# Gating bias written by ScalarE into reserved PSUM banks, a small gain table and unread products at the start, merge weights called three steps sooner, residual rows in another buffer

## The chip, the cores and the metric

One Trainium2 chip, 8 cores, one program on all of them. Each core takes one prompt sequence of 2048 positions and 16 sample sequences of 4 positions (64 rows); no core talks to another. The metric is the device time in microseconds of the slowest core. The kernel before took 1095.3 us (median of three runs).

## The reference, cut to what matters

```
xn = rmsnorm(h) * g_mix
proj = xn @ w_in                       # mixer A pair | u, v of mixer B | branch gates
glu = a_val * sigmoid(a_gate);  ca = causal depthwise conv (width 31) of glu
y_a = silu(layernorm(ca)) @ w_a_out
u, v = gelu(proj_u), gelu(proj_v)
v_n = layernorm(v) * ln_b_g + ln_b_b
s[t] = sum_s W_s[head][t, s] * v_n[s] + b_s[head][t]     # 128-position chunks, s <= t
y_b = (u * s) @ w_b_out
h = h + (sigmoid(g_a) * y_a + sigmoid(g_b) * y_b) @ w_out
h = h + ConvFFN(rmsnorm(h));  y = rmsnorm(h)
```

The outputs are y for prompt and sample rows, the carried convolution rows, and v_n of the sample rows (`o_vs`).

## The kernel before, in words

Everything on a core lives in one SBUF array (`arena`) with hand-set offsets; PSUM (`ps`) is eight banks, handed out in rotation by `rbank`. A small scheduler class writes one instruction list per engine, in program order, with semaphore waits where a buffer or bank is reused; so each engine is strictly first in, first out, and the order of the Python calls is the order on each queue. Weights (`w_all`, f32 in memory, bf16 in SBUF) come by DMAs that GpSimd issues; x, small tables and outputs by DMAs that SyncE issues. Every matmul is recorded under L303 (`mm`), every transpose under L313 (`tr`), ACTIVATE under L321, sum of squares under L318, two-tensor products under L324, tensor-scalar under L329 and L331, the three-input form under L334, DMAs under L180.

The stages in order of time:

- **Normalise and u.** 17 chunks of rows (16 of 128, the sample chunk of 64 is number 16). For each c: `sq` on ScalarE (needs x of c), `xscale` of c-1 on VectorE, `sq_rstd` of c (VectorE, then a power on GpSimd), transposes of c-1 on TensorE and `norm_evac` of c-1 on VectorE, which multiplies by the gain column 34 of the table `colA` (148 KB, loaded by SyncE after the second x). `PLAN[c]` says which u products (first column, width, column block j) run in step c; they need block j of the u weights and the normalised chunks.
- **v and the spatial mix.** Chunk 16 first, then 0 to 15. `v_mm` has 16 products of 512 columns and two Gelus into `vt` (f32); `v_stats` takes mean and 1/deviation; `v_center` is (v - mean) * gain on VectorE; `v_scale` on ScalarE multiplies by 1/deviation into `vn` (bf16). Two steps later `v_mix` puts the bias `Bm` into a bank by a product with the identity (512 columns, `start=True`), adds four products of 128 columns for four heads, twice per chunk, and VectorE multiplies u by the bank. `BmS` is the bias of the sample chunk, in one bank.
- **GLU** (32 steps of 16 products), with the sample rows' convolution on VectorE between.
- **Convolution.** For i = 0 to 15: for i below 8 a transposing step, then `conv(i)` (48 products of 128 columns, split over two banks) with coefficient matrices that `t_build` makes on GpSimd, ScalarE and VectorE three steps ahead; VectorE evacuates. `mload(4)` at i = 7 has GpSimd issue the loads of the first four merge blocks, gate and weight of mixer B for j = 0 and 1. They go to the last quarter of `Xc` (byte 25344 on), which conv(0) to conv(3) read. At i = 9, 11, 13 and 15 `run_fill(1)` runs one merge tile (`half_b`: 8 gate products, 8 weight products). From i = 8 on VectorE also takes LayerNorm statistics (`q_half`).
- **LayerNorm and transposes of mixer A** (`q_stats`, `q_z`, `q_tr`, with Silu on ScalarE), then the **merge** over j, then **w_out** (`wo_mm`): 17 chunks, each 16 products of 512, residual addition on VectorE with x rows in `xr` (three buffers at `OFF_C`, loaded by `xr_load`), sum of squares, scaling (`n2_scale`), and two steps later the transposes (`n2_tr`). The bytes of `xr` lie in `tbuf`, which the merge uses to its end. `u` (at `OFF_B`) is last read by `half_b` of j = 7.
- **ConvFFN** (22 blocks up, then down) and final norm, from 620 us to the end.

## Time and profile before

| what | value |
|---|---|
| median of the runs (lowest, highest) | 1095.3 us (1095.11, 1096.93) |
| the profiled execution's own time | 1095.86 us |
| its span, slowest core | 1094.2 us (cores: 1090.3 to 1094.2) |
| TensorE busy | 1064.1 us (97%) |
| VectorE, ScalarE, GpSimd busy | 630.7, 438.2, 181.4 us |
| mean granted TensorE clock, cores | 0.996 to 0.998 |

How to read it: all rows are of core 0, the slowest. PE is TensorE, PEld its weight loads, DVE VectorE, ACT ScalarE, POOL GpSimd, SPq the DMA issues of SyncE. In a timeline row the numbers are start and length in us, then engine, line, operation, output <- input, shape and count; the bracket says how long the engine had been idle before the first of them and what it waited for.

### The profile page before, as it was taken

To read this page: it belongs to the slowest core of one execution; us is meant where nothing else is said; L and a number is where in the kernel's file an instruction comes from. 1 tells how busy PE (TensorE), PEld (TensorE's weight loads), DVE (VectorE), ACT (ScalarE), POOL (GpSimd) and SP (SyncE) were. 2 spreads that over 40 slices of the span, in tenths; PEclk is the share of its full clock that TensorE was granted. 3 is DMA by queue.
4 is the path that set the end of the run, shared out by engine and by line. 5 is a ranking of instruction groups with operands and counts; after the bars stand their busy time and mean duration, and the time that the engine had idled before them with its cause. 6 is when DMAs were issued, how large, how long until landed. Compare 5 with 4: busy or idle time off the path is not lost.

```text
span 1094.2 us, 19114 instructions; the slowest of 8 cores (1090.3 to 1094.2 us)
## 1 busy us (share of the span) xinstructions
PE 1064.1 (97%) x6621; PEld 610.2 (56%) x6621; DVE 630.7 (58%) x1256; ACT 438.2 (40%) x800; POOL 181.4 (17%) x376
## 2 busy tenths in 40 slices
PE   5999999999899999999999999999999999999997
PEld 4764456666765555555545455555555555444444
DVE  4556987695988333333446666666666666333233
ACT  4644441123737411111155555555555555210111
POOL 3241113150631000100011111111111111000000
PEclk9999999999999999999999999999999999999999
DMA  9979014010240222142288623333223322543331
GB/s 211 268 102 166 1 26 87 2 30 1 35 78 2 40 39 37 28 73 39 49 248 273 175 40 58 59 58 50 50 50 56 59 49 40 138 145 116 116 109 65
DMA packets 36365, 89.40 MB, mean 82 GB/s; under 512 B 4080, under 2 KB 6256, under 8 KB 36272
## 3 DMA queue, kind: packets, MB, share of 16 engines
q0 software_dynamic: 21488, 38.74, 22.4%
q1 hardware_dynamic: 14784, 49.45, 14.0%
q8 instruction: 54, 0.88, 0.3%
q14 instruction: 39, 0.32, 0.1%
HBM read 108.57 MB, written 20.04 MB: 118 GB/s over the span
## 4 chain that ended last, share of the span: by engine, by line
PE 92%; DMA 2%; DVE 2%; ACT 1%; issue 1%; POOL 1%; SPq 0%; POOLq 0%; DVEq 0%; ACTq 0%
PE ps L303 90%; PE ps L313 2%; DMA arena<-x_p 2%; ACT arena L321 1%; DVE arena L334 1%; ACT arena L318 1%; DMA arena<-w_all 0%; POOL arena L331 0%; DVE arena L324 0%; DVE arena L604 0%; POOL arena L324 0%; SPq L180 0%; DVE arena L331 0%; DVEq L194 0%; POOLq L262 0%
## 5 line engine op out<-in xcount | busy, mean ns | idle before, releaser
L303 PE MATMUL ps<-arena 128*128 128x512 bf16 (+6 forms) x6077 | 1039.2, 334 | 9.6 <-DMA arena<-w_all 3.7
L303 PEld LDWEIGHTS ps<-arena 128*128 128x128 bf16 (+1 forms) x6077 | 577.6, 102 | 454.0 <-issue 20.5
L321 ACT ACTIVATE arena<-ps 128x512 f32<-128x512 f32 (+7 forms) x362 | 180.8, 513 | 295.0 <-PE ps L303 214.2
L334 DVE SCALAR_TENSOR_TENSOR arena<-arena 128x64 f32<-128x64 bf16 (+5 forms) x538 | 255.7, 511 | 34.6 <-POOL arena L324 14.5
L321 ACT ACTIVATE arena<-arena 128x512 f32<-128x512 f32 (+5 forms) x179 | 118.3, 673 | 195.5 <-DVE arena L334 171.9
L334 DVE SCALAR_TENSOR_TENSOR arena<-arena,ps 128x512 f32<-128x512 f32 (+4 forms) x120 | 69.9, 588 | 156.8 <-PE ps L303 147.8
L324 DVE TENSOR_TENSOR arena<-arena,ps 128x512 bf16<-128x512 f32 (+2 forms) x143 | 86.6, 615 | 83.9 <-ACT arena L321 83.5
L318 ACT ACTIVATE arena<-arena 128x1024 bf16<-128x1024 f32 (+3 forms) x53 | 54.2, 1022 | 152.4 <-DVE arena L324 132.9
L324 DVE TENSOR_TENSOR arena<-ps,arena 128x1024 bf16<-128x1024 bf16 (+4 forms) x71 | 64.0, 905 | 74.2 <-PE ps L303 66.5
L180 POOL DMA_DIRECT2D arena<-w_all x138 | 74.2, 549 | 192.1 <-PE ps L303 178.1
L321 ACT ACTIVATE arena<-ps,arena 128x512 f32<-128x512 f32 (+3 forms) x150 | 101.2, 705 | 4.4 <-PE ps L313 4.4
L324 POOL TENSOR_TENSOR arena<-arena 128x1 f32<-128x1 f32 (+2 forms) x73 | 42.1, 577 | 350.6 <-DVE arena L331 254.1
L331 DVE TENSOR_SCALAR arena<-arena 128x1 f32<-128x1 f32 (+4 forms) x81 | 25.4, 333 | 77.6 <-ACT arena L318 74.6
L331 POOL TENSOR_SCALAR arena<-arena 128x384 bf16<-128x384 bf16 x82 | 47.4, 596 | 96.1 <-PE ps L303 84.8
L341 POOL COPY arena<-arena 128x32 f32<-128x32 f32 (+1 forms) x66 | 13.9, 212 | 260.5 <-ACT arena L321 256.2
L313 PE MATMUL ps<-arena 128*128 128x128 bf16 (+2 forms) x544 | 40.9, 222 | 13.8 <-DVE arena L329 9.1
L313 PEld LDWEIGHTS ps<-arena 128*128 128x128 bf16 (+2 forms) x544 | 35.0, 100 | 23.0 <-issue 16.4
L334 DVE SCALAR_TENSOR_TENSOR arena<-ps,arena 128x512 f32<-128x512 f32 (+1 forms) x72 | 43.2, 642 | 5.1 <-DMA arena<-x_p 3.3
L324 DVE TENSOR_TENSOR arena<-arena 128x512 bf16<-128x512 f32 (+8 forms) x51 | 30.5, 597 | 8.4 <-ACT arena L321 2.2
L604 DVE BATCH_NORM_STATS2 arena<-arena 128x6 f32<-128x512 f32 (+1 forms) x34 | 23.5, 690 | 7.6 <-ACT arena L321 5.8
L329 DVE TENSOR_SCALAR arena<-arena 128x1024 bf16<-128x1024 f32 (+6 forms) x54 | 21.8, 413 | 4.6 <-POOL arena L324 2.3
L806 DVE BATCH_NORM_STATS2 arena<-arena 128x6 f32<-128x512 f32 (+1 forms) x34 | 21.4, 679 | 0.1
(17 smaller groups left out, 28.2 us busy)
## 6 DMA issues: line engine op xcount, KB each, us to landing
arena<-w_all POOLq DMA_DIRECT2D x138, 256.0 KB, 5.2
arena<-x_p SPq DMA_DIRECT2D x32, 512.0 KB, 7.4
h1s<-arena SPq DMA_DIRECT2D x16, 512.0 KB, 3.8
arena<-h1s SPq DMA_DIRECT2D x16, 512.0 KB, 4.2
o_yp<-arena SPq DMA_DIRECT2D x15, 512.0 KB, 2.9
o_ch<-st_a SPq DMA_DIRECT2D x1, 1664.0 KB, 18.7
arena<-dw_t POOLq DMA_DIRECT2D x4, 384.0 KB, 9.3
arena<-st_a POOLq DMA_DIRECT2D x1, 960.0 KB, 12.7
```

Source lines behind the costliest of these rows:

```text
L180: e.items.append(("op", lambda q, o=out, i=in_: q.dma_start(out=o, in_=i), stream, 16))
L303: S.op("pe", lambda q: q.matmul(out, lhsT=lhsT, rhs=rhs, start=start, stop=stop), [out], [lhsT, rhs], inc=stop)
L313: S.op("pe", lambda q: q.transpose(out=out, in_=in_, identity=ident), [out], [in_, ident], inc=inc)
L318: S.op("act", lambda q: q.activation(out=out, in_=in_, func=func, scale=scale, bias=bias, accum_out=accum), [out, accum], ins)
L321: S.op("act", lambda q: q.activation(out=out, in_=in_, func=func, scale=scale, bias=bias), [out], ins)
L324: S.op(en, lambda q: q.tensor_tensor(out=out, in0=in0, in1=in1, op=op), [out], [in0, in1])
L329: S.op(en, lambda q: q.tensor_scalar(out=out, in0=in0, scalar1=s1, scalar2=None, op0=op0), [out], ins)
L331: S.op(en, lambda q: q.tensor_scalar(out=out, in0=in0, scalar1=s1, scalar2=s2, op0=op0, op1=op1), [out], ins)
L334: S.op("dve", lambda q: q.scalar_tensor_tensor(out=out, in0=in0, scalar=scalar, in1=in1, op0=op0, op1=op1), [out], [in0, in1] + ([scalar] ...
L341: S.op(en, lambda q: q.tensor_copy(out=out, in_=in_), [out], [in_])
L604: S.op("dve", lambda q, i=i, a=a: q.bn_stats(out=s[:cs, 6 * i:6 * i + 6], in_=a), [s[:cs, 6 * i:6 * i + 6]], [a])
L806: S.op("dve", lambda e: e.bn_stats(out=s[:cs, 6 * hf:6 * hf + 6], in_=src[:cs]), [s[:cs, 6 * hf:6 * hf + 6]], [src[:cs]])
```

## The change

It does five things. The gain of the first norm comes from a table of its own, `colG` (4 KB), loaded second; `colA` follows the first eight x chunks. `warm(n)` puts n products of 128 columns of the identity into a bank that nobody reads, at five places of the first steps, and four u products of width 256 (block 2 to 5, columns 0 on) move one step later in `PLAN`. In the v stage `v_center` is gone: ScalarE does (v * rstd - mean * rstd) in place, GpSimd makes -mean * rstd and multiplies by the gain (`v_gain`), ScalarE writes the bias into a bank (`v_pre`; the first four by TensorE), banks 4 to 7 are kept for this and `rbank` turns over 0 to 3, the mix runs three steps behind instead of two, and the last three mixes stand among the first GLU steps. `vt` and `vn` turn by position in the order. The load of `b_dw` moves behind the last mix, so that of the carried rows `o_ch` no longer stands behind it. `mload(4)` is called at i = 4. `xr` moves from `OFF_C` to `OFF_B`.

```diff
...
     col_a = din("col_a", (128, 8, 37))
+    col_g = din("col_g", (128, 8, 1))
     col_f = din("col_f", (128, NFF, 4))
...
+        banks = [list(range(8))]
         def rbank():
-            b = bank_rr[0] % 8
+            b = banks[0][bank_rr[0] % len(banks[0])]
             bank_rr[0] += 1
...
-        def mm(out, lhsT, rhs, start, stop):
-            S.op("pe", lambda q: q.matmul(out, lhsT=lhsT, rhs=rhs, start=start, stop=stop), [out], [lhsT, rhs], inc=stop)
+        def mm(out, lhsT, rhs, start, stop, onto=False, inc=None):
+            S.op("pe", lambda q: q.matmul(out, lhsT=lhsT, rhs=rhs, start=start, stop=stop, skip_group_check=onto), [out], [lhsT, rhs],
+                 inc=stop if inc is None else inc)
...
         o += 384
+        colG = view(o, F32, (128, 8, 1))
+        o += 64
         M8 = view(o, F32, (128, 8))
...
         u_load()
-        xload(1)
+        S.dma("sp", colG, col_g)
+        for c in range(1, NXB):
+            xload(c)
         S.dma("sp", colA, col_a)
-        for c in range(2, NXB):
-            xload(c)
         mset(nh, -0.5)
...
-        def norm_evac(c, gcol):
+        def norm_evac(c, gcols):
             cs = rows(c)
             tt("dve", xnT[:, :, c * 128:c * 128 + cs], psb(nbank[c], BF16)[:, 0:8 * cs].rearrange("p (k t) -> p k t", k=8),
-               colA[:, :, gcol:gcol + 1].broadcast_to([128, 8, cs]), ALU.mult)
+               gcols.broadcast_to([128, 8, cs]), ALU.mult)
...
             xtr(c - 1)
-            norm_evac(c - 1, 34)
+            norm_evac(c - 1, colG)
...
             2: [(0, A1, (0, 1))],
-            3: [(128, A1, (0, 1)), (0, A2, (2,))],
-            4: [(0, A2, (3,)), (256, A1, (0, 1))],
-            5: [(384, A1, (0, 1)), (256, A2, (2,)), (0, A2, (4,))],
-            6: [(256, A2, (3, 4)), (0, A2, (5,))],
-            7: [(512, A2, (0, 1, 2))],
+            3: [(128, A1, (0, 1))],
+            4: [(256, A1, (0, 1)), (0, A2, (2,))],
+            5: [(384, A1, (0, 1)), (256, A2, (2,)), (0, A2, (3,))],
+            6: [(256, A2, (3,)), (0, A2, (4,)), (256, A2, (4,))],
+            7: [(512, A2, (0, 1, 2)), (0, A2, (5,))],
             8: [(0, A2, (6, 7)), (256, A2, (5, 6))],
...
         }
+        def warm(n):
+            b = rbank()
+            for i in range(n):
+                mm(psb(b)[:, 0:128], ident_b, ident_b, i == 0, i == n - 1)
         nstep(0)
...
         xscale(0)
+        warm(40)
         nstep_pe(1)
         sq_rstd(1)
+        warm(12)
         for c in range(2, 18):
...
                 u_mm(*p_)
+                if (c, n) == (2, 0):
+                    warm(18)
                 if n == 0:
                     nstep_pe(c)
+                if (c, n) in ((2, 1), (3, 1)):
+                    warm(12)
                 if c == 17:
...
         vstat = {}
+        vidx = {c: (c + 1) % 17 for c in CHUNKS}
...
                 for q in range(2):
-                    act(vt[c % 3][:64, q * 512:(q + 1) * 512], psb(b)[64 * q:64 * q + 64, :], AF.Gelu)
+                    act(vt[vidx[c] % 3][:64, q * 512:(q + 1) * 512], psb(b)[64 * q:64 * q + 64, :], AF.Gelu)
             for q in range(2) if c < 16 else ():
...
                     mm(psb(b)[:cs, :], xnT[:, k, c * 128:c * 128 + cs], vW[k][:, q * 512:(q + 1) * 512], k == 0, k == 7)
-                act(vt[c % 3][:cs, q * 512:(q + 1) * 512], psb(b)[:cs, :], AF.Gelu)
+                act(vt[vidx[c] % 3][:cs, q * 512:(q + 1) * 512], psb(b)[:cs, :], AF.Gelu)
...
             vstat[c] = s
-            t = vt[c % 3][:cs]
+            t = vt[vidx[c] % 3][:cs]
             layer_stats(s, [t[:, 0:512], t[:, 512:1024]], cs)
             layer_rstd(s, cs)
-        def v_center(c):
-            cs = rows(c)
-            s = vstat[c]
-            t = vt[c % 3][:cs]
-            stt(t, t, s[:cs, 12:13], lnbg[:cs], ALU.subtract, ALU.mult)
+            tsc("pool", s[:cs, 16:17], s[:cs, 12:13], s[:cs, 15:16], -1.0, ALU.mult, ALU.mult)
...
             cs = rows(c)
-            act(vn[c % 3][:cs], vt[c % 3][:cs], AF.Identity, scale=vstat[c][:cs, 15:16])
+            t = vt[vidx[c] % 3][:cs]
+            s = vstat[c]
+            act(t, t, AF.Identity, scale=s[:cs, 15:16], bias=s[:cs, 16:17])
+        def v_gain(c):
+            cs = rows(c)
+            t = vt[vidx[c] % 3][:cs]
+            tt("pool", vn[vidx[c] % 3][:cs], t, lnbg[:cs], ALU.mult)
             if c == 16:
-                stt(vso, vt[c % 3][:cs], vstat[c][:cs, 15:16], lnbb, ALU.mult, ALU.add)
+                tt("dve", vso, t, lnbg[:cs], ALU.mult)
+                tt("dve", vso, vso, lnbb, ALU.add)
                 S.dma("sp", o_vs, vso)
+        MB = [4, 5, 6, 7]
+        mbank = {}
+        mcount = [0]
+        def v_pre(c):
+            mbank[c] = []
+            for hf in range(2 if c < 16 else 1):
+                b = MB[mcount[0] % 4]
+                bias = Bm[:, 4 * hf:4 * hf + 4, :] if c < 16 else BmS
+                if mcount[0] < 4:
+                    mm(psb(b), ident_b, bias, True, True)
+                else:
+                    cp("act", psb(b).rearrange("p (a b) -> p a b", a=4 if c < 16 else 8), bias)
+                mcount[0] += 1
+                mbank[c].append(b)
         def v_mix(c):
-            cs = rows(c)
             if c < 16:
-                for hf in range(2):
-                    b = rbank()
-                    mm(psb(b), ident_b, Bm[:, 4 * hf:4 * hf + 4, :], True, False)
+                for hf, b in enumerate(mbank[c]):
                     for h4 in range(4):
...
                         o_ = psb(b)[:, h4 * 128:(h4 + 1) * 128]
-                        mm(o_, vn[c % 3][:, hd * 128:(hd + 1) * 128], WsT[:, hd, :], False, h4 == 3)
+                        mm(o_, vn[vidx[c] % 3][:, hd * 128:(hd + 1) * 128], WsT[:, hd, :], False, True, True, h4 == 3)
                     uu = u[:, 4 * hf:4 * hf + 4, c * 128:(c + 1) * 128]
...
             else:
-                b = rbank()
-                mm(psb(b), ident_b, BmS, True, False)
+                b = mbank[c][0]
                 for hd in range(8):
                     o_ = psb(b)[:, hd * 64:(hd + 1) * 64]
-                    mm(o_, vn[c % 3][:64, hd * 128:(hd + 1) * 128], WsTb[:, hd, :], False, hd == 7)
+                    mm(o_, vn[vidx[c] % 3][:64, hd * 128:(hd + 1) * 128], WsTb[:, hd, :], False, True, True, hd == 7)
                 uu = u[:, :, 2048:2112]
...
         order = [16] + list(range(16))
+        banks[0] = [0, 1, 2, 3]
         for i in range(len(order)):
...
             v_stats(order[i])
+            if i >= 1:
+                v_gain(order[i - 1])
+            if i >= 3:
+                v_mix(order[i - 3])
             if i >= 2:
-                v_mix(order[i - 2])
-            v_center(order[i])
+                v_pre(order[i - 2])
...
         gluS = view(OFF_D + 32768 + 8704, F32, (128, 8, 96))
-        S.dma("sp", bdw, b_dw.partition_broadcast(128))
         S.dma("sp", o_ch, st_a[:, :, 64:480])
...
+        glu(0)
+        v_pre(order[15])
+        v_scale(order[16])
+        v_gain(order[16])
+        v_mix(order[14])
         s_glu(1, (0,))
-        v_scale(order[16])
-        glu(0)
         v_mix(order[15])
+        v_pre(order[16])
         glu(1)
         v_mix(order[16])
+        bank_rr[0] %= 4
+        banks[0] = list(range(8))
+        S.dma("sp", bdw, b_dw.partition_broadcast(128))
         s_glu(1, (1,))
...
                 q_half(16, 1)
-            if i == 7:
+            if i == 4:
                 mload(4)
...
-        xr = [view(OFF_C + 4096 * i, F32, (128, D)) for i in range(3)]
+        xr = [view(OFF_B + 4096 * i, F32, (128, D)) for i in range(3)]
         h1 = [view(OFF_C + 12288 + 4096 * i, F32, (128, D)) for i in range(3)]
...
             trans8(xs2[i % 3], rows(c), nbank[c])
-            norm_evac(c, 35)
+            norm_evac(c, colA[:, :, 35:36])
...
         "col_a": np.ascontiguousarray(col.reshape(37, 8, 128).transpose(2, 1, 0)),
+        "col_g": np.ascontiguousarray(f(inp["g_mix"]).reshape(8, 128, 1).transpose(1, 0, 2)),
         "col_f": np.ascontiguousarray(colf.reshape(4, NFF, 128).transpose(2, 1, 0)),
```

## Rows read from the trace of the kernel before

**Rows 1.** The page, part 4: the chain that ended last, by engine.

```profile
PE 92%; DMA 2%; DVE 2%; ACT 1%; issue 1%; POOL 1%; SPq 0%; POOLq 0%; DVEq 0%; ACTq 0%
```

**Rows 2.** Waits of TensorE over the whole span: total us, times, longest us.

```profile
PE ps L313 <- ACT arena L321: 4.1, 3, 1.7
```

**Rows 3.** Timeline of the first 32 us, core 0.

```profile
7.73 1.06 ACT L318 ACTIVATE arena<-arena 128x1024 bf16<-128x1024 f32 x1 [1.39 <-DMA arena<-x_p]
...
10.54 1.23 DVE L324 TENSOR_TENSOR arena<-ps,arena 128x1024 bf16<-128x1024 bf16 x1 [2.22 <-DMA arena<-col_a]
...
13.86 1.06 ACT L318 ACTIVATE arena<-arena 128x1024 bf16<-128x1024 f32 x1 [4.98 <-DMA arena<-x_p]
...
17.36 1.06 ACT L318 ACTIVATE arena<-arena 128x1024 bf16<-128x1024 f32 x1 [1.60 <-DMA arena<-x_p]
...
18.25 3.38 PE L303 MATMUL ps<-arena 128*128 128x128 bf16 x24
...
30.59 1.03 PE L303 MATMUL ps<-arena 128*128 128x256 bf16 x8 [0.21 <-DVE arena L324]
```

**Rows 4.** Groups by shape, 110 to 140 us: busy us, mean ns, idle.

```profile
L303 PE MATMUL ps<-arena 128*128 128x512 bf16 x124 | 29.2, 379 | 0.0
...
L334 DVE SCALAR_TENSOR_TENSOR arena<-arena 128x1024 f32<-128x1024 f32 x7 | 8.9, 1278 | 0.0
...
L321 ACT ACTIVATE arena<-arena 128x1024 bf16<-128x1024 f32 x7 | 8.0, 1148 | 16.0 <-DVE arena L334 16.0
...
L321 ACT ACTIVATE arena<-ps 128x512 f32<-128x512 f32 x14 | 7.4, 582 | 0.0
```

**Rows 5.** Timeline of the v stage, ScalarE.

```profile
118.31 1.15 ACT L321 ACTIVATE arena<-arena 128x1024 bf16<-128x1024 f32 x1 [2.29 <-DVE arena L334]
...
122.71 1.15 ACT L321 ACTIVATE arena<-arena 128x1024 bf16<-128x1024 f32 x1 [2.29 <-DVE arena L334]
```

**Rows 6.** Groups of equal shape on GpSimd, whole span.

```profile
L331 POOL TENSOR_SCALAR arena<-arena 128x384 bf16<-128x384 bf16 x82 | 47.4, 596 | 96.1 <-PE ps L303 84.8 <-DMA arena<-dw_t 11.1
...
L324 POOL TENSOR_TENSOR arena<-arena 128x1 f32<-128x1 f32 x64 | 35.3, 551 | 304.0 <-DVE arena L331 241.5 <-DVE arena L329 62.5
```

**Rows 7.** Timeline of the convolution, 286 to 301 us.

```profile
286.19 0.58 POOL L180 DMA_DIRECT2D arena<-dw_t  x1 [0.60 <-ACT arena L321]
...
289.62 5.26 POOL L331 TENSOR_SCALAR arena<-arena 128x384 bf16<-128x384 bf16 x9 [2.86 <-PE ps L303]
...
294.83 2.17 POOL L180 DMA_DIRECT2D arena<-w_all  x4
...
300.29 5.89 PE L303 MATMUL ps<-arena 128*128 128x512 bf16 x27 [3.71 <-DMA arena<-w_all]
```

**Rows 8.** Window: busy (count) PE, PEld, DVE, ACT, POOL, clock, DMA, GB/s.

```profile
300.30:303.60 3.30, 3.30 (x8) 1.12 (x9) 1.99 (x4) 0.00 (x0) 0.09 (x1) 0.50 0.99 163
```

**Rows 9.** Timeline after the first merge tile, VectorE.

```profile
305.67 0.69 DVE L334 SCALAR_TENSOR_TENSOR arena<-arena,ps 128x512 f32<-128x512 f32 x1 [3.37 <-PE ps L303]
...
324.53 0.45 DVE L334 SCALAR_TENSOR_TENSOR arena<-arena,ps 128x288 f32<-128x288 f32 x1 [0.64 <-PE ps L303]
...
329.27 2.98 DVE L331 TENSOR_SCALAR arena<-arena 128x1024 bf16<-128x1024 f32 x4 [0.60 <-POOL arena L324]
```

**Rows 10.** Timeline of the w_out stage.

```profile
551.41 1.22 DVE L324 TENSOR_TENSOR arena<-arena 64x1024 f32<-64x1024 f32 x1 [2.17 <-ACT arena L321]
...
557.39 1.29 DVE L334 SCALAR_TENSOR_TENSOR arena<-ps,arena 128x512 f32<-128x512 f32 x2 [3.27 <-DMA arena<-x_p]
...
562.26 0.61 PE L313 MATMUL ps<-arena 128*128 128x128 bf16 x8 [1.45 <-ACT arena L321]
...
578.31 3.62 PE L303 MATMUL ps<-arena 128*128 128x512 bf16 x16
...
582.21 3.62 PE L303 MATMUL ps<-arena 128*128 128x512 bf16 x16
...
615.31 0.61 PE L313 MATMUL ps<-arena 128*128 128x128 bf16 x8 [1.74 <-ACT arena L321]
```

## The prediction

> **What bounds the kernel now.** First the page's chain that ended last [rows 1]: 92% of it is TensorE, so a change pays where it removes TensorE work or one of its few waits. Then the waits of TensorE and the timelines around them. There are four places. In the first 30 us x arrives late and the products run at half speed [rows 3]. In the v stage TensorE never waits [rows 4]; a chunk takes 122.71 - 118.31 = 4.40 us [rows 5], so only less TensorE work helps. In the convolution it stands still 3.71 us for the first merge block, and the next products run at half clock [rows 7, 8]. In the w_out stage it waits for ScalarE, 1.45 us at the start and 1.74 at the end [rows 10]; with one of 0.9 these make the 4.1 us of [rows 2]. A gain in one place can be eaten by the next engine in line; below I ask for it each time.
>
> **Front.** x of chunk 1 is there at 7.73, of chunk 2 at 13.86, of chunk 3 at 17.36 [rows 3]: an x takes 3.5 us, yet 6.13 lie between 1 and 2, so the table between them costs 2.6 us, and VectorE waited for it until 10.54. In these steps `norm_evac(c-1)` stands behind `sq_rstd(c)` on VectorE and so behind x of c. With `colA` last, x 2 to 7 come up to 2.6 us sooner. Against that, `colG` goes ahead of x 1: it costs between nothing and the same 2.6; it has as many rows of 32 bytes instead of 1184, and no weight load runs beside it yet, so I take 0.4. The product at 30.59, the first of step 7, waited for this chain and comes about 2.2 us sooner. But a product of width 256 and 8 blocks was moved into step 7. Eight products of 512 took 3.30 us at half clock [rows 8], 0.41 each, 0.21 at full clock, so the moved one is 8 x 0.1 = 0.9 us. Left: **1.3 us** (0 to 1.7). The loads of all eight x and `colA` are the same bytes, so x 8 comes no sooner, and the later steps are TensorE's own. On SyncE `colG` adds one issue before x 1.
> The 94 unread products cost 0.05 us each at full clock (a quarter of 0.21) and 0.10 at half, 5 to 10 us of TensorE, all in time in which it would wait for x: forty before the first transposes, the others in gaps of about a microsecond each. Their cover is the 3.5 us rhythm of x against some 1.4 us of work in steps 2 and 3. What they buy is speed: the 24 products from 18.25 are 4096 columns in 3.38 us, 1.2 columns per ns, the 1.2 GHz level. At 2.4 they take half, which matters only where TensorE and not x is late; so I count no gain for it, but without it the 2.2 us would shrink, since slow products would then be what x waits for.
>
> **v stage.** Removed: 33 bias products of 512 columns, four of which come back: 29. A chunk is 18 products of 512 and 8 of 128 in 4.40 us. A w_out chunk is 16 of 512 and 8 transposes of 128 in 582.21 - 578.31 = 3.90 [rows 10]. That is the new chunk, so a bias product is worth 0.25; by its columns alone 0.21. I take 0.235: 29 x 0.235 = **6.8 us** (6.1 to 7.3). Does another engine become the bound at 3.90?
> VectorE loses `v_center`, 1.28 per chunk [rows 4]: free.
> ScalarE has two Gelus of 0.58, `v_scale` 1.15 (same row, now into f32), and two bias writes of 512, nearest row the Gelu of 512, 0.58: 3.5 of 3.90. It holds until a bias write costs 0.8.
> GpSimd is the unknown. It has the power, 0.55 [rows 6], the new 128x1 product (at most the power's 0.55, I take 0.25), some 0.3 between instructions, and the gain product of 1024 f32 elements, of which no row exists. Below: 0.6 for 384 elements with one input [rows 6], in proportion 1.6 for 1024, or 1.3 if half of the 0.6 is fixed. Above: twice 1.6, for two inputs: 3.2. I take the middle, 2.2, so GpSimd is busy 3.3 of 3.90. The limit is 3.90 - 1.1 = 2.8.
> The Trainium skill, GPSIMD Engine Reference, § 3.1, gives a two-input f32 product 1.96 times VectorE's time; with VectorE's 1.22 for 1024 [rows 10] that would be 2.4, as an estimate, and the sum would not change.
> The added waits: the mix waits for GpSimd's product, which has the slack of the third step; the bias write waits for VectorE's multiply of the mix two chunks before, done a chunk earlier; behind it on ScalarE stands the next Gelu, with 0.4 us to spare. Four banks for `v_mm` are two chunks' worth. The tail (mixes among GLU steps) has one GLU step of cover for each. `o_ch` runs at the start of the stage instead of its end, beside GLU weights that are not needed before the stage is over: nothing. The second VectorE product for the sample rows (1.22) lies in VectorE's free time: nothing.
>
> **Merge blocks.** GpSimd idles 2.86 us until 289.62, after the coefficient load issued at 286.19 [rows 7]. conv(3) has by then been read, so the four issues, 2.17 us, go from 286.8 to 289.0: they fit, and no build is late. The load took 300.29 - 294.83 = 5.5 us to be usable; behind the coefficient load I allow 8 us: 295. The tile is due when conv(9) ends, 300.29 - 3.71 = 296.6. Gone then: 3.71 of wait, and the half clock: eight products in 3.30 where full clock needs 1.65 [rows 8]. Together 5.4. What is late next is VectorE: its evacuations run without pause up to the tile, and the first thing it could skip is its wait of 3.37 before 305.67 [rows 9], then small ones such as the 0.64 before 324.53. The LayerNorm products at 329.27 hang on that chain, and the transposes after them and Silu on ScalarE on these. So the gain is between 3.4 and 5.4; VectorE's rows give 3.4 + 0.6 + something: **4.3 us**. GpSimd's 2.17 us also leave the place between two builds.
>
> **Residual.** The first x rows were waited for 3.27 us by VectorE at 557.39 [rows 10]; their issue stood behind the last use of `tbuf`. `u` is free three columns of `half_a` sooner (j = 5, 6, 7), so all three loads land while the merge runs. The wait of 1.45 before 562.26 goes. The loop of evacuation, square, scale, transpose turned at TensorE's 3.90 with no slack, so the delay was carried to the end and came out as the 1.74 before 615.31: that goes too, but for about 0.2, since the last transpose follows scaling with only half a step between. **3.0 us** (1.5 to 3.2).
>
> **Sum.** 1.3 + 6.8 + 4.3 + 3.0 = 15.4. From the profiled execution's own 1095.86 (span 1094.2): 1080.5. The median of the runs is 0.6 lower, so **1080.0**.
>
> **Rivals.**
> *GpSimd bounds the v stage.* For: its product has no row, and it has only 0.6 us to spare. Against: 0.6 for 384 elements. At the upper bound of 3.2 a chunk takes 4.3, and 16 x 0.4 = 6.4 come back: 1086.4. Chance 0.10.
> *Slower than before: the same product, held up.* If it takes 4.6 us, a chunk takes 5.7 instead of 4.40, 16 x 1.3 = 21 us lost; with the 8.6 of the other parts, 1095 + 21 - 9 = 1107. It decides from a product of about 3.8 (chunk 4.9) on. The Trainium skill, SBUF — State Buffer, § Who interferes with whom, says that VectorE instructions with two SBUF inputs or in a two-port mode lock GpSimd out for their whole length. This is such a mechanism; here VectorE's mix reads one input from PSUM and its statistics have one input, so little would lock. The trace: nine GpSimd pieces beside VectorE's own pieces of the same builds took 5.26, 0.584 each, no more than the mean of 0.596 [rows 6, 7]. Chance 0.04.
> *VectorE eats the merge gain*, or the clock falls all the same: 2 instead of 4.3 us, 1082.3. Chance 0.09.
> *The early call does not load earlier* (the issues wait for something else, or land behind the coefficients after 300): 1084.3. Chance 0.04.
> *The front gives nothing or costs* (unread products in the way, u weights late): up to 2 us more than before, 1083.3. Chance 0.08.
> The forecast: 0.65.
>
> **Range and chances.** The low end has every upper bound: 1.7 + 7.3 + 5.4 + 3.2 = 17.6, and a little for what I left out, 1077.0. The high end takes in GpSimd as the bound: 1087.0. A measurement of this kernel tells about 0.2% (2 us) from no change. Faster 0.94, same 0.02 (the worst of the first rival's 0.10), slower 0.04 (the second rival).
>
> **What would show it.** v stage: chunk of 3.9 us, GpSimd product of 2 to 2.5, TensorE without a pause; wrong if TensorE waits for GpSimd or ScalarE. Convolution: no wait for `w_all`, clock 1.00 all through, GpSimd's four issues before the build of 289.62; wrong if a pause appears before conv(10) or the first `q_tr`. w_out: no VectorE wait for x, no TensorE wait of over 0.3. Front: x 2 at about 11.6, first product of step 7 near 28.4; wrong if TensorE waits for u weights there.

## The result, and the profile after

| | before | after |
|---|---|---|
| median of the runs | 1095.4 us | 1081.1 us |
| ratio, 95% interval | | 0.9865 [0.9847, 0.9882] |
| profiled execution, own time | 1095.86 us | 1081.38 us |
| spans of the cores | 1090.3 to 1094.2 us | 1078.6 to 1079.8 us |

The medians here and below are over all executions, slow ones in which the cores of one die ran at a lower granted clock included (one of after took 1111.6 us, the four others 1080.6 to 1081.4 with 1080.8 in the middle), while the ratios are of the undisturbed ones alone. The forecast was 1080.0 us, in a range of 1077 to 1087; by the median it was 1.1 us too low, by the 1080.8 it was 0.8. So 14.3 to 14.6 us were won where 15.4 were expected. The parts came out less evenly than their sum. Line numbers moved: `mm` is L306 now, `tr` L317, ACTIVATE L325, sum of squares L322, two-tensor products L328, tensor-scalar L333 and L335, the three-input form L338. In the kernels of the experiments they can be one to three lower.

The page of after (core 2, its slowest): the span, the busy times, and the chain that ended last.

```profile
span 1079.8 us, 19303 instructions; the slowest of 8 cores (1078.6 to 1079.8 us)
PE 1054.8 (98%) x6597; PEld 612.3 (57%) x6686; DVE 617.8 (57%) x1240; ACT 454.7 (42%) x829; POOL 227.3 (21%) x410
PE 93%; issue 2%; DVE 1%; DMA 1%; POOL 1%; ACT 1%; SPq 0%; POOLq 0%; DVEq 0%; ACTq 0%
```

TensorE still makes the chain [rows 1]. ScalarE is busy 16 us more and GpSimd 46 more, both beside it. The waits of TensorE on core 0, whole span (total us, times, longest us), against [rows 2]:

```profile
PE ps L306 <- DVE arena L345: 3.5, 1, 3.5
PE ps L317 <- ACT arena L325: 1.8, 2, 0.9
PE ps L306 <- DMA arena<-w_all: 0.5, 1, 0.5
```

The 3.5 is the very start, until the identity exists. The waits for ScalarE fell from 4.1 to 1.8, and the 3.71 for merge weights is gone (the 0.5 left is of u weights in the front).

**Where the time went.** Five marks cut an execution into stretches. In after, core 0, they are the first 64-row statistics, the first 24 products of the convolution, the table loads of Silu and of Gelu, and the issue for `st_f` at the end of w_out:

```profile
85.85 1.47 DVE L623 BATCH_NORM_STATS2 arena<-arena 64x6 f32<-64x512 f32 x2 [5.82 <-ACT arena L325]
319.81 1.28 ACT L325 ACT_TABLE_LOAD   x1 [2.94 <-PE ps L317]
534.64 1.28 ACT L325 ACT_TABLE_LOAD   x1
600.52 0.42 SPq L180 DMA_DIRECT2D arena<-st_f  x1
```

The mark between the first two is at 270.11 us. The same marks on all eight cores of each kernel give (means, lowest and highest core in brackets; the first column starts at 0, so it is the front):

| kernel | front | v and GLU | convolution to Silu | w_out | span, mean (highest) |
|---|---|---|---|---|---|
| before | 86.3 (85.7 to 86.9) | 191.57 | 53.85 (52.2 to 54.8) | 67.2 (66.7 to 68.4) | 1092.0 (1094.2) |
| after | 86.0 (85.9 to 86.2) | 184.35 (184.23 to 185.05) | 49.70 | 65.9 | 1078.9 (1079.8) |
| v stage alone | 86.4 (85.9 to 87.3) | 184.76 | 53.5 (51.5 to 55.1) | 68.2 (67.2 to 69.3) | 1086.4 (1089.5) |
| merge call alone | 86.9 (85.8 to 87.7) | 191.57 | 49.69 | 67.6 (66.9 to 68.8) | 1088.7 (1089.7) |
| residual rows alone | 86.6 (85.8 to 87.0) | 191.58 | 53.2 (51.9 to 55.2) | 65.5 | 1089.9 (1092.3) |
| front alone | 86.2 (85.7 to 86.7) | 191.63 | 53.7 (51.7 to 55.9) | 67.4 (65.7 to 69.0) | 1091.9 (1094.2) |
| all but the v stage | 86.9 (86.2 to 88.3) | 191.64 | 49.7 (49.7 to 50.0) | 65.55 | 1086.8 (1088.2) |
| before, gap filled | 86.8 (86.2 to 87.6) | 191.57 | 53.1 (52.6 to 53.9) | 67.2 (66.2 to 67.7) | 1091.6 (1093.4) |
| after, bias by TensorE | 86.7 (86.2 to 87.3) | 190.19 | 49.7 | 65.9 | 1085.4 (1086.1) |
| after, gain on VectorE | 86.8 (86.3 to 88.2) | 190.50 | 49.7 | 65.5 | 1085.5 (1086.8) |
| after, no unread products | 86.7 (86.3 to 87.1) | 184.23 | 49.7 | 65.9 | 1079.5 (1080.1) |
| after, plan of before | 86.9 (86.2 to 87.4) | 184.24 | 49.7 | 65.9 | 1079.6 (1080.1) |
| after, two-input product added | 86.8 (86.5 to 87.1) | 185.40 | 49.7 | 65.9 | 1080.7 (1081.0) |
| after, GpSimd's product twice | 86.7 (85.8 to 87.2) | 217.9 (217.3 to 218.9) | 49.7 | 65.9 | 1113.1 (1114.4) |

The merge, 214.8 us, and the rest after w_out, 478.1, are not in the table: they are the same in every kernel, but for the rest on three cores of "v stage alone", where it is 479.8.

Two things are to be seen. A stretch in which TensorE waits for no DMA has mostly one length on all eight cores, to some hundredths (v and GLU nearly everywhere; convolution and w_out wherever the edit is in). A stretch with such a wait differs by 2 to 4 us from core to core. And the metric is the slowest core, which in before was the one with the longest waits, core 0: on it the stretches give 0.70 + 7.31 + 5.05 + 2.47 = 15.5 us (forecast 15.4), on the mean of the cores 0.3 + 7.2 + 4.15 + 1.3 = 13.0. The slowest core of after is another one, core 2, so the result is 14.4 in spans.

Core 2 of after is an exception to the first: seven cores have 184.23 to 184.26 in v and GLU, and core 2 has 185.05. The view of its GLU steps shows what happened. VectorE's, GpSimd's and TensorE's timelines, core 2:

```profile
216.69 9.29 DVE L338 SCALAR_TENSOR_TENSOR arena<-arena 128x64 f32<-128x64 bf16 x1
```

```profile
216.87 9.03 POOL L335 TENSOR_SCALAR arena<-arena 128x384 bf16<-128x384 bf16 x16
```

```profile
227.70 5.37 PE L306 MATMUL ps<-arena 128*128 128x512 bf16 x23 [0.62 <-DVE arena L338]
```

One VectorE piece of 64 elements took 9.29 us and ended 0.08 after sixteen pieces of GpSimd that ran without a pause. The same pieces take some 0.6 us on core 0 beside the same row of GpSimd's. VectorE's evacuation came late, and TensorE waited 0.62 for it. On the 32 cores of before, after, "bias by TensorE" and "no unread products" this is the only piece of the GLU steps from 200 to 236 us that took over 2 us. What let it happen on one core wasn't tried.

### The profile page after: what moved, and what is told of

It reads as the page before. It is cut to its first block, busy times and chain, and to the rows that moved or that the text cites. A ratio compares the mean times of both kernels' runs of the same rounds, so it can differ in the third digit from the quotient of the medians.

```text
span 1079.8 us, 19303 instructions; the slowest of 8 cores (1078.6 to 1079.8 us)
## 1 busy us (share of the span) xinstructions
PE 1054.8 (98%) x6597; PEld 612.3 (57%) x6686; DVE 617.8 (57%) x1240; ACT 454.7 (42%) x829; POOL 227.3 (21%) x410
## 3 DMA queue, kind: packets, MB, share of 16 engines
q1 hardware_dynamic: 14928, 49.46, 14.6%
## 4 chain that ended last, share of the span: by engine, by line
PE 93%; issue 2%; DVE 1%; DMA 1%; POOL 1%; ACT 1%; SPq 0%; POOLq 0%; DVEq 0%; ACTq 0%
PE ps L306 90%; PE ps L317 3%; DMA arena<-x_p 1%; DVE arena L338 1%; ACT arena L325 1%; DVE arena L328 0%; POOL arena L335 0%; POOL arena L328 0%; ACT arena L322 0%; DVE arena L335 0%; SPq L180 0%; DVE arena L623 0%; POOLq L263 0%; DVEq L194 0%; DVE arena L345 0%
## 5 line engine op out<-in xcount | busy, mean ns | idle before, releaser
L306 PE MATMUL ps<-arena 128*128 128x512 bf16 (+6 forms) x6053 | 1029.8, 331 | 13.9 <-DVE arena L328 3.5
L306 PEld LDWEIGHTS ps<-arena 128*128 128x128 bf16 (+1 forms) x6142 | 580.7, 102 | 446.4 <-issue 12.8
L325 ACT ACTIVATE arena<-ps 128x512 f32<-128x512 f32 (+7 forms) x362 | 182.1, 514 | 301.7 <-PE ps L306 220.8
L338 DVE SCALAR_TENSOR_TENSOR arena<-arena 128x64 f32<-128x64 bf16 (+4 forms) x520 | 238.5, 494 | 32.9 <-POOL arena L328 13.0
L325 ACT ACTIVATE arena<-arena 128x512 f32<-128x512 f32 (+6 forms) x179 | 119.8, 681 | 158.1 <-DVE arena L338 133.5
L338 DVE SCALAR_TENSOR_TENSOR arena<-arena,ps 128x512 f32<-128x512 f32 (+4 forms) x120 | 69.7, 587 | 148.4 <-PE ps L306 140.9
L328 POOL TENSOR_TENSOR arena<-arena 128x1 f32<-128x1 f32 (+3 forms) x90 | 83.1, 925 | 296.5 <-DVE arena L335 251.5
L328 DVE TENSOR_TENSOR arena<-arena,ps 128x512 bf16<-128x512 f32 (+2 forms) x143 | 86.6, 615 | 83.9 <-ACT arena L325 83.9
L322 ACT ACTIVATE arena<-arena 128x1024 bf16<-128x1024 f32 (+3 forms) x53 | 54.2, 1022 | 151.8 <-DVE arena L328 132.9
L328 DVE TENSOR_TENSOR arena<-ps,arena 128x1024 bf16<-128x1024 bf16 (+4 forms) x71 | 64.0, 905 | 72.8 <-PE ps L306 65.8
L325 ACT ACTIVATE arena<-ps,arena 128x512 f32<-128x512 f32 (+3 forms) x150 | 101.2, 705 | 4.4 <-PE ps L317 4.4
L335 POOL TENSOR_SCALAR arena<-arena 128x384 bf16<-128x384 bf16 (+2 forms) x99 | 52.4, 545 | 96.9 <-PE ps L306 83.6
L335 DVE TENSOR_SCALAR arena<-arena 128x1 f32<-128x1 f32 (+4 forms) x81 | 25.8, 336 | 79.5 <-ACT arena L322 75.8
L317 PE MATMUL ps<-arena 128*128 128x128 bf16 (+2 forms) x544 | 40.1, 219 | 4.4 <-ACT arena L325 1.8
L338 DVE SCALAR_TENSOR_TENSOR arena<-ps,arena 128x512 f32<-128x512 f32 (+1 forms) x72 | 42.9, 640 | 1.8 <-PE ps L306 1.7
L317 PEld LDWEIGHTS ps<-arena 128*128 128x128 bf16 (+2 forms) x544 | 34.1, 98 | 14.1 <-issue 7.3
L328 DVE TENSOR_TENSOR arena<-arena 128x512 bf16<-128x512 f32 (+8 forms) x53 | 32.9, 621 | 8.7 <-ACT arena L325 2.2
L333 DVE TENSOR_SCALAR arena<-arena 128x1024 bf16<-128x1024 f32 (+6 forms) x54 | 21.8, 412 | 4.7 <-POOL arena L328 2.3
```

The lines of the kernel that those rows point to most:

```text
L306: S.op("pe", lambda q: q.matmul(out, lhsT=lhsT, rhs=rhs, start=start, stop=stop, skip_group_check=onto), [out], [lhsT, rhs], inc=stop if i ...
L317: S.op("pe", lambda q: q.transpose(out=out, in_=in_, identity=ident), [out], [in_, ident], inc=inc)
L322: S.op("act", lambda q: q.activation(out=out, in_=in_, func=func, scale=scale, bias=bias, accum_out=accum), [out, accum], ins)
L325: S.op("act", lambda q: q.activation(out=out, in_=in_, func=func, scale=scale, bias=bias), [out], ins)
L328: S.op(en, lambda q: q.tensor_tensor(out=out, in0=in0, in1=in1, op=op), [out], [in0, in1])
L333: S.op(en, lambda q: q.tensor_scalar(out=out, in0=in0, scalar1=s1, scalar2=None, op0=op0), [out], ins)
```

## The experiments

**One part at a time.** Four kernels from before, each with one part of the change as the diff ahead of the prediction shows it: the v stage, the call of `mload(4)`, the place of `xr`, and the front (`colG`, unread products, plan).

```diff
-            if i == 7:
+            if i == 4:
                 mload(4)
...
-        xr = [view(OFF_C + 4096 * i, F32, (128, D)) for i in range(3)]
+        xr = [view(OFF_B + 4096 * i, F32, (128, D)) for i in range(3)]
```

> The kernel before with the v stage alone changed (ScalarE bias writes, GpSimd gain product, kept banks, mixes three steps behind and spread, b_dw later). Main theory: each bias product taken from TensorE is worth 0.25 us, 29 of them 7.2 us, on every core alike, since no DMA is in it: about 1088.2, chunk of 3.9 us. Rival (the v stage's gain needs the earlier front, or part of it is given back in the GLU stage by VectorE): under 5 us, above 1090.5.

> The kernel before with the first merge loads called at i = 4 instead of 7. Theory A (the wait of 3.7 us and the half clock are the same on all cores): every core gains 5.0, 1090.4. Theory B (how long a load takes differs from core to core, so that the wait is a different one on each; in the kernel before the stretch from the first convolution to the Silu table took 52.2 to 54.8 us by core): the cores end up alike at 49.7 in that stretch, the mean gains 4.2, the slowest about 5; the time is between 1090.4 and 1091.5 and the spread of the cores' spans shrinks.

> The kernel before with the residual rows in the place of u. Theory A: both waits of ScalarE go on every core, 2.5 to 3 us: 1092.5. Theory B (only the cores whose x rows came latest had long waits; the stretch from the Gelu table to the load of the FFN history took 66.7 to 68.4 us by core): the stretch is 65.9 on all, the mean gains 1.3, core 0 gains 2.5; time 1093 to 1094.

> The kernel before with the front alone changed (small table, order of loads, unread products, four u products later). Main theory: x 2 comes 1 us sooner and the moved product takes 0.9 back: start of the v stage 0.3 us earlier in the mean of the cores, 0.7 on core 0; time 1095.0, no difference to be measured. Rival (the front is worth the 1.3 forecast): 1094.1.

Each set of experiments was run beside executions of before of its own (medians 1096.1 to 1097.0), so a time is to be read by its ratio.

| alone | median | ratio, 95% interval |
|---|---|---|
| v stage | 1091.6 us | 0.9956 [0.9938, 0.9974] |
| merge call | 1091.5 us | 0.9955 [0.9940, 0.9971] |
| residual rows | 1094.4 us | 0.9986 [0.9976, 0.9996] |
| front | 1096.0 us | 1.0001 [0.9991, 1.0011] |

The merge call and the residual rows do what their theories B said: their stretch gets one length on all cores (49.7, 65.5), and the mean gains less than core 0 does. The front alone moves nothing.

The v stage took its stretch from 191.57 to 184.76, 6.8 us on every core, near the 7.2 of its main theory, and yet only 0.44% off the time, 4.8 us, which is what the rival said. The other stretches tell why. On the mean of the cores w_out is 1.0 us longer than in before (68.2 for 67.2). TensorE's wait near its end is 2.1 us on seven of the cores, where before has 1.7 on all, and on three of these seven, cores 1, 2 and 3, the clock fell behind it. TensorE's timeline of the v stage alone, core 3, its slowest:

```profile
608.96 0.61 PE L316 MATMUL ps<-arena 128*128 128x128 bf16 x8 [2.08 <-ACT arena L324]
609.41 5.30 PE L305 MATMUL ps<-arena 128*128 128x512 bf16 x16
```

Sixteen products took 5.30 us where they take 3.62 [rows 10], and the granted clock of 610 to 613 us is 0.50. That is the 1.65 by which the rest after w_out is longer on these three cores. From core 0 of before to core 3 of this kernel the stretches give -6.8 in v and GLU, +0.7 in the front, +0.3 in the convolution, -0.6 in w_out and +1.6 behind it: -4.7, the 4.7 of the slowest spans (1094.2 to 1089.5). Why the wait near the end of w_out is longer with the v stage of after wasn't tried.

The single parts sum to 1.02% (11 us) where together they make 1.35%. With intervals of 0.1 to 0.2% on each the gap of 0.33% is itself only about as large as its uncertainty.

**All but the v stage.** Before, with the front, the merge call and the residual rows.

```diff
+        colG = view(o, F32, (128, 8, 1))
...
+            3: [(128, A1, (0, 1))],
...
-            if i == 7:
+            if i == 4:
                 mload(4)
...
-        xr = [view(OFF_C + 4096 * i, F32, (128, D)) for i in range(3)]
+        xr = [view(OFF_B + 4096 * i, F32, (128, D)) for i in range(3)]
```

> Before, with all parts of the change but that of the v stage: front, merge blocks, residual rows. It asks why the parts, each made alone, sum to 10.8 us where together they give 14.3. Theory A: the time is that of the slowest core, and each core waits for its DMAs by another amount; a part alone leaves the waits of the others, which pick another core as the slowest. With all three in, the cores end within about 1.5 us of each other, and the three are worth more than the 6.2 us of the single runs: 0.3 + 4.15 + 1.3 off the mean of the cores (1092.0) and the spread of 2.2 us above that mean gone to 0.9: 1087.1 span, 7.1 us, about 1088.3 us, ratio 0.9935, and 7.2 above after. Theory B: the v stage made alone meets something that it doesn't meet in after, and the others simply add: 6.2 us, ratio 0.9943, 1089.2.

1089.9 us, ratio 0.9937 [0.9924, 0.9951]. The interval holds both 0.9935 and 0.9943, so the time doesn't decide. The trace bears out a part of theory A: convolution and w_out have one length on the cores (49.7, one core 50.0, and 65.55), and the spread of the spans falls from 3.9 to 1.9 us. But the three single ratios sum to 0.58% and this kernel makes 0.63%, so these three simply add, as theory B says. What is worth more in company is the v stage: 0.44% alone, 0.72% as the difference between this kernel and after. In mean spans that is 5.6 us alone and 7.9 in company. In company its stretch gives 7.3, the front 0.9 (86.9 against 86.0, which no part of the v stage touches), and w_out takes 0.3 back. Alone, w_out and the fallen clock behind it took back 1.6. So theory B is right in this too: made alone, the v stage meets something that it doesn't meet in after, a wait of 2.1 near the end of w_out, which is 0.9 there.

**The bias by TensorE again.** After, one line changed.

```diff
-                if mcount[0] < 4:
+                if True:
                     mm(psb(b), ident_b, bias, True, True)
```

> After, with the bias of every chunk of the v stage written by the product with the identity again (29 more products of 512 columns); all else of the v stage (centring on ScalarE, gain on GpSimd, kept banks, the mix three steps behind, three mixes among the GLU steps) stays. Main theory: only the number of products sets the chunk, 29 x 0.235 to 0.25 = 6.8 to 7.3 us more, so 1088 us, ratio to before 0.993, the chunk 4.36 to 4.40 us, ScalarE with 1.2 us less per chunk. Rival: part of the 7.2 us that this stretch gained comes from the other edits (order, banks, the moved centring); then the time stays below 1086.

1087.8 us, ratio 0.9916 [0.9901, 0.9931]. That is 0.51% above after, 5.6 us; the stretch is 5.9 longer on seven cores and 5.1 on core 2, the one with the late piece in after. ScalarE's timeline in this kernel, core 0, gives the chunk:

```profile
115.44 1.23 ACT L325 ACTIVATE arena<-arena 128x1024 f32<-128x1024 f32 x1
119.77 1.23 ACT L325 ACTIVATE arena<-arena 128x1024 f32<-128x1024 f32 x1
```

4.33, and 4.33 to the next at 124.10. Against 3.90 in after that is 0.43 for two bias products, 0.22 each, close to the 0.21 by columns; 29 of them would be 6.3. Of the 0.4 missing from that, 0.13 is a pause between 150 and 155 us that after has and this kernel hasn't; the rest I didn't trace. So 5.9 of the 7.3 us of this stretch on core 0 are the products. The other 1.4 us, before's 191.57 against 190.19, come from the rest of the edit: before's chunk was 4.40 with the same count of products. TensorE's weight loads in before show a gap in each chunk:

```profile
118.01 1.18 PEld L303 LDWEIGHTS ps<-arena 128*128 128x128 bf16 x6
119.57 3.38 PEld L303 LDWEIGHTS ps<-arena 128*128 128x128 bf16 x23 [0.38 <-issue]
```

and this kernel has none there:

```profile
117.94 5.08 PEld L306 LDWEIGHTS ps<-arena 128*128 128x128 bf16 x30
```

16 x 0.07 us would be 1.1 of the 1.4. Which edit closes the gap (the kept banks, the mix three steps behind, the other order) wasn't tried alone. The time of 1088 is that of the main theory; the rival was right in that not all of the gain is the count of products, though not in its number, under 1086.

**The gain on VectorE.** After, with the product by the gain moved from GpSimd.

```diff
-            tt("pool", vn[vidx[c] % 3][:cs], t, lnbg[:cs], ALU.mult)
+            tt("dve", vn[vidx[c] % 3][:cs], t, lnbg[:cs], ALU.mult)
```

> The changed kernel with the gain product on VectorE instead of GpSimd. Main theory: VectorE then has 3.4 + 1.25 us per chunk, more than TensorE's 3.90, so a chunk takes 4.6 to 4.7 and the stage 16 x 0.75 = 12 us longer: 1093. Rival (the third step of slack hides it): 1081.

1088.4 us, ratio 0.9919 [0.9902, 0.9937]. The chunk is 4.35 (ScalarE's scaling at 112.59, 116.94 and 121.28), where the main theory had 4.6 to 4.7 and twice the loss: VectorE has 3.1 us of other work in a chunk, not 3.4. VectorE is the bound: its timeline over one chunk, core 0, is full,

```profile
114.35 0.21 DVE L626 BATCH_NORM_AGGREGATE arena<-arena 128x2 f32<-128x12 f32 x1
114.67 0.15 DVE L333 TENSOR_SCALAR arena<-arena 128x1 f32<-128x1 f32 x1
114.77 1.23 DVE L328 TENSOR_TENSOR arena<-arena 128x1024 bf16<-128x1024 f32 x1
115.92 1.28 DVE L328 TENSOR_TENSOR arena<-arena,ps 128x512 bf16<-128x512 bf16 x2
117.11 1.48 DVE L623 BATCH_NORM_STATS2 arena<-arena 128x6 f32<-128x512 f32 x2
```

0.21 + 0.15 + 1.23 + 1.28 + 1.48 = 4.35. And GpSimd's power, 0.55 in [rows 6], stands beside the product with both inputs in SBUF:

```profile
114.97 1.43 POOL L328 TENSOR_TENSOR arena<-arena 128x1 f32<-128x1 f32 x1 [2.48 <-DVE arena L333]
```

It began 0.2 us into that product and ended 0.4 after it. Giving GpSimd the product is what makes 3.90 possible; against VectorE it is worth 6.2 us of this stretch.

**GpSimd's product twice.** This goes at the rival that ended slower than before.

```diff
-            tt("pool", vn[vidx[c] % 3][:cs], t, lnbg[:cs], ALU.mult)
+            for _ in range(2):
+                tt("pool", vn[vidx[c] % 3][:cs], t, lnbg[:cs], ALU.mult)
```

> The changed kernel with the GpSimd gain product done twice. It measures from where on GpSimd bounds the stage, the second rival of the prediction. Main theory: GpSimd has 2 x 2.36 + 0.55 + 0.27 + 0.3 = 5.8 us per chunk, a chunk takes 5.8, the stage 16 x 1.9 = 30 us longer: 1111. Rival (other waits come on top, buffers of vt turning too slowly): over 1120.

1116.5 us, ratio 1.0181 [1.0159, 1.0203]. TensorE's timeline, core 0, then GpSimd's (two products and one power in a group of three):

```profile
122.23 4.06 PE L306 MATMUL ps<-arena 128*128 128x128 bf16 x23 [1.69 <-POOL arena L328]
```

```profile
117.13 5.35 POOL L328 TENSOR_TENSOR arena<-arena 128x1024 bf16<-128x1024 f32 x3
122.88 5.35 POOL L328 TENSOR_TENSOR arena<-arena 128x1024 bf16<-128x1024 f32 x3
```

A chunk takes 122.88 - 117.13 = 5.75, and TensorE stands still 1.7 in each. The mechanism of the rival is real: it had 5.7 for a product of 4.6 us, and with 4.7 us the kernel is slower than before by 20 us. Its turning point at 3.8 lies between the 2.36 and the 4.7 and wasn't measured. The time came between what the two theories say. On core 0 the stretch is 33.4 us longer than in after. TensorE's sixteen waits for GpSimd sum to 29.9 us. Each costs some 0.16 more than the wait itself (a chunk grows by 1.85, the wait is 1.7), together about 2.4. And behind the last and longest, 3.77, the granted clock is 0.68 from 185 to 190 us, which costs 1.6.

**A product with two SBUF inputs beside GpSimd's.** After, with an unread product on VectorE in each chunk.

```diff
             tt("pool", vn[vidx[c] % 3][:cs], t, lnbg[:cs], ALU.mult)
+            tt("dve", view(OFF_D + 65536, F32, (128, 256)), lnbg[:, 0:256], lnbg[:, 256:512], ALU.mult)
```

> After, with one unread product of 256 columns with both inputs in SBUF on VectorE for each chunk of the v stage (some 0.35 us, so VectorE has 3.5 of 3.9 busy). It asks whether GpSimd stands still beside such an instruction. If it does, GpSimd's product of 2.36 us, or the power of 0.55 if that is beside it, takes about 0.35 us longer, and both stay as they are if not. In either case TensorE has no wait and the time stays at 1081, since GpSimd then has 3.6 of 3.9 busy.

1082.6 us, one run; the chunk stays at 3.90. In the steady chunks the piece fell between GpSimd's instructions: the power took 0.59 to 0.60 instead of 0.55, the product 2.37. There the case tells nothing. At the start of the stage they met. GpSimd's timeline, core 0, and VectorE's:

```profile
93.34 2.35 POOL L328 TENSOR_TENSOR arena<-arena 64x1024 bf16<-64x1024 f32 x1
...
99.87 3.05 POOL L328 TENSOR_TENSOR arena<-arena 128x1024 bf16<-128x1024 f32 x2
```

```profile
93.41 3.35 DVE L328 TENSOR_TENSOR arena<-arena 64x1024 f32<-64x1024 f32 x1 [0.17 <-DVE arena L328]
...
100.95 1.55 DVE L328 TENSOR_TENSOR arena<-arena 128x256 f32<-128x256 f32 x1
...
120.39 0.41 DVE L328 TENSOR_TENSOR arena<-arena 128x256 f32<-128x256 f32 x1
```

The product of the sample rows takes 1.22 in after; begun 0.07 after GpSimd's, it took 3.35, 2.28 until GpSimd's end and nearly its own time after. The piece of 256 took 1.55 beside GpSimd's product and 0.41 alone. So here it isn't GpSimd that loses but whichever began second, and it loses the whole rest of the other's instruction. The delay went through: TensorE waited 1.32 us for GpSimd at 102.37, against 0.32 in after, 1.0 of the 1.14 us by which the stretch grew on core 0. The Trainium skill, SBUF — State Buffer, § Who interferes with whom, states this rule both ways (whoever issues first holds the shared pair for the whole instruction); this trace and the 1.43 above agree. I had expected GpSimd to lose here, and 0.35 us; wrong in direction and size.

**The gap filled.** Before, with 60 unread products of the identity ahead of the first merge tile, so that the wait stays and the clock doesn't fall. The 60 products add nothing to the output.

```diff
+            if i == 9:
+                unread(60)
             if i in (9, 11, 13, 15):
                 run_fill(1)
```

> The kernel before with 60 unread products of 128 columns (3.4 us) between conv(9) and the first merge tile, so that TensorE works while it waits for the blocks; the loads stay at i = 7. Theory A (the wait costs twice, 3.7 us of standing and 1.65 of half clock behind it): the eight products from about 300 run at clock 1.00, the Silu table comes about 1.6 us sooner (stretch from the first convolution 52.2 in the mean instead of 53.85), time 1094.3 to 1095. Theory B (VectorE is late anyway, so the clock costs nothing): the clock is full and the stretch is unchanged.

1095.5 us, ratio 0.9991 [0.9981, 1.0000]. The windows of this kernel, core 0 (engine busy times; then PEclk, DMA share, GB/s):

```profile
300.00:304.00 4.00, 3.95 (x29) 2.11 (x28) 2.80 (x6) 0.60 (x1) 0.55 (x1) 1.00 1.00 121
```

The clock is 1.00 where [rows 8] has 0.50, and the tile is evacuated at 303.65 instead of 305.67 [rows 9]. Yet the time falls by about 1 us, at most 2, and the stretch, 53.1 on the mean of the cores, is between the 52.2 of theory A and the 53.85 of theory B. All cores of the five kernels with the late call tell why. Core 6 of before waited for the same load; its timeline and its window:

```profile
300.43 3.78 PE L303 MATMUL ps<-arena 128*128 128x512 bf16 x19 [3.49 <-DMA arena<-w_all]
```

```profile
300.40:303.70 3.30, 3.27 (x16) 1.53 (x17) 2.25 (x5) 0.60 (x1) 0.34 (x1) 1.00 1.09 140
```

Almost the same pause as on core 0 (3.49 for 3.71), the same 3.30 us, but 16 products at the 2.4 GHz level where core 0 has eight at 1.2. Its convolution stretch is 3.17 us longer than the 49.70 of after, core 0's is 5.05. In before and the three single-part kernels with the late call, 32 cores in all:

| clock in the 3.3 us after the pause | cores | pause | stretch over 49.70, less the waits for `w_all`: median (lowest, highest) |
|---|---|---|---|
| 0.50 to 0.69 | 19 | 2.3 to 4.2 us | +1.35 (+1.1 to +2.5) |
| 1.00 | 13 | 2.2 to 3.5 us | -0.34 (-0.6 to +0.7) |

On six of the cores with the full clock a second, short wait of 0.2 to 0.7 us for the next block follows; it is taken off too. So a pause that leaves the clock alone costs 0.34 less than its length, and a fall of the clock costs 1.7 on top, the 1.65 that [rows 8] holds. VectorE swallows nothing beyond that 0.34. How long the pause was doesn't by itself say which happens, since the two kinds overlap from 2.3 to 3.5 us. The 60 products take 3.2 us themselves: in this kernel four cores stand at 2.86 over after without any wait, the others at 3.4 to 4.2 with one of 0.4 to 1.0. They help the cores whose clock would have fallen and cost the others something, and the slowest core gains little.

**No unread products.** After, `warm` doing nothing.

```diff
             b = rbank()
-            for i in range(n):
+            for i in range(0):
```

> The changed kernel without any unread product. Theory A (they give the first 20 us the full clock, and it matters): the first transposes take 1.0 us instead of 0.6, products fall behind x, the v stage starts 1 us or more later: 1082 to 1083. Theory B (x is the bound and the half-clock products fit between its arrivals): v stage starts within 0.3 us of 86.0: 1081.1.

1081.8 us, ratio 0.9865 [0.9849, 0.9880], the ratio of after itself. Timeline of TensorE, core 0, of this kernel, then of after:

```profile
8.47 1.01 PE L317 MATMUL ps<-arena 128*128 128x128 bf16 x8 [8.47 <-DVE arena L333]
...
16.59 1.06 PE L317 MATMUL ps<-arena 128*128 128x128 bf16 x8
...
29.82 1.03 PE L306 MATMUL ps<-arena 128*128 128x256 bf16 x8 [0.96 <-DVE arena L328]
```

```profile
8.47 0.61 PE L317 MATMUL ps<-arena 128*128 128x128 bf16 x8 [0.58 <-DVE arena L333]
...
16.05 0.61 PE L317 MATMUL ps<-arena 128*128 128x128 bf16 x8
...
29.02 1.03 PE L306 MATMUL ps<-arena 128*128 128x256 bf16 x8 [0.18 <-DVE arena L328]
```

The unread products do what they are for: the first three transposing steps take 0.4 us less each, 0.61 for 1.01. The prediction took products at half rate for the 1.2 GHz level by the 1.2 columns per ns; the granted clock of the profile reads 1.00 here in before, in this kernel and in after, so it does not bear that out, and what halves the rate stays open. But the v stage starts at 86.7 here and, in the seven kernels with after's whole front (the doubled product too), at 86.0, 86.2, 86.7, 86.7, 86.8, 86.8 and 86.9: no difference that this measurement can tell.

**The plan of before.** After, with `PLAN[3]` to `PLAN[7]` of before.

```diff
-            3: [(128, A1, (0, 1))],
-            4: [(256, A1, (0, 1)), (0, A2, (2,))],
+            3: [(128, A1, (0, 1)), (0, A2, (2,))],
+            4: [(0, A2, (3,)), (256, A1, (0, 1))],
...
-            7: [(512, A2, (0, 1, 2)), (0, A2, (5,))],
+            7: [(512, A2, (0, 1, 2))],
```

> After, with the plan of the u products of before (four groups of eight products of width 256 one step earlier, so one group less in step 7). Main theory (the 0.9 us that the prediction charges for the moved group): TensorE waits for x in steps 2 to 6 of after by 0.4 to 1.0 us in each, the group of width 256 fits there, and the products from step 7 on, which run without a pause, are eight fewer: the v stage starts 0.8 to 0.9 us sooner on every core, 1080.2 us. Rival: the weights of block 2 and the following ones are not there yet one step sooner, TensorE waits for them with the transposes behind it, and the start of the v stage stays or comes up to 2 us later, 1081 to 1083.

1081.7 us, ratio 0.9859 [0.9840, 0.9879]. The rival was right. TensorE's timeline, core 0:

```profile
17.12 2.15 PE L306 MATMUL ps<-arena 128*128 128x128 bf16 x28
20.24 1.03 PE L306 MATMUL ps<-arena 128*128 128x256 bf16 x8 [0.97 <-DMA arena<-w_all]
21.11 0.61 PE L317 MATMUL ps<-arena 128*128 128x128 bf16 x8
```

The weights of block 2 land at 20.2, TensorE waits 0.97 for them with a transpose behind, and the start of the v stage stays (86.9 mean). So the early place gives nothing with x coming sooner, and the late one costs nothing that can be measured; in before x was so late that TensorE never waited for these weights.

## Why the prediction was right

**v stage, 6.8 forecast, 7.2 on the mean, 7.3 on core 0.** The steady state came as worked out. GpSimd's timeline of after, core 0:

```profile
119.45 2.36 POOL L328 TENSOR_TENSOR arena<-arena 128x1024 bf16<-128x1024 f32 x1
122.41 0.55 POOL L328 TENSOR_TENSOR arena<-arena 128x1 f32<-128x1 f32 x1 [0.59 <-DVE arena L333]
123.35 2.36 POOL L328 TENSOR_TENSOR arena<-arena 128x1024 bf16<-128x1024 f32 x1
```

The chunk is 123.35 - 119.45 = 3.90; the product 2.36 where I took 2.2, a bias write 0.59 against 0.58, and GpSimd has 0.7 us to spare. The Trainium skill, GPSIMD Engine Reference, § 3.1, has its 1.96 from an addition; by it the estimate was 2.4, and this trace agrees, 2.36 against 1.22 to 1.23 on VectorE. TensorE of core 0 waits once in the v stage, 0.32 for GpSimd at the start. What failed is the size of one term: a bias product is worth 0.22, not 0.235, and 1.4 us come from edits to which I gave nothing. I had read the 4.40 of [rows 5] as all columns, though the weight loads pause 0.38 us in it. The two errors partly cancel. One bound was mis-worked without harm: half of 0.6 fixed and the rest in proportion is 1.1 us for 1024 elements, not 1.3. That GpSimd could be held up I had put down to VectorE's mix reading PSUM; right for the steady chunks, wrong for the two products of the sample rows, which I had put in VectorE's free time at no cost: in after GpSimd's power beside them took 1.59, and TensorE's wait of 0.32 for GpSimd follows. That the one makes the other is argued, not tried. Nor did I think of VectorE being the one held up, as on core 2 in the GLU steps.

**Merge blocks, 4.3 forecast, 5.05 on core 0, 4.15 on the mean.** GpSimd's timeline, core 0:

```profile
278.19 0.58 POOL L180 DMA_DIRECT2D arena<-dw_t  x1 [0.60 <-ACT arena L325]
278.77 2.13 POOL L180 DMA_DIRECT2D arena<-w_all  x4
281.60 6.97 POOL L335 TENSOR_SCALAR arena<-arena 128x384 bf16<-128x384 bf16 x12 [0.70 <-PE ps L306]
```

The four issues stand in the idle 2.86 us of [rows 7], as forecast, and no build is late. TensorE then runs in one piece, and VectorE doesn't wait for the first tile as it did for 3.37 us [rows 9]:

```profile
287.06 30.73 PE L306 MATMUL ps<-arena 128*128 128x128 bf16 x280 [0.67 <-POOL arena L335]
```

```profile
302.30 1.27 DVE L852 BATCH_NORM_STATS2 arena<-arena 128x6 f32<-128x512 f32 x2
303.50 1.27 DVE L338 SCALAR_TENSOR_TENSOR arena<-ps,arena 128x512 f32<-128x512 f32 x2
```

The step that failed is "VectorE's rows give 3.4 + 0.6 + something". I took VectorE for the next limit; it isn't, and both terms of the upper bound came nearly whole on core 0: 3.71 of pause and 1.65 of clock, less 0.34, are 5.02, and 5.05 was measured. Where the clock of before hadn't fallen, on cores 6 and 7, the gain is 3.2 and 2.5. The mean of 4.15 lies near the 4.3 by that mixture, not by my reason.

**Residual rows, 3.0 forecast, 2.47 on core 0, 1.3 on the mean.** The wait of VectorE [rows 10] is gone. What stayed is TensorE's wait near the end, which I had let fall to 0.2 and which, at over 0.3, was one of my own signs of being wrong; timeline of after, core 0:

```profile
599.78 0.61 PE L317 MATMUL ps<-arena 128*128 128x128 bf16 x8 [0.87 <-ACT arena L325]
```

I read it as the chain of evacuation, square, power and scaling of the last chunk, which doesn't fit into the products between, however early x comes; no run tried that. It isn't the delay of x carried on, as I had it: in before the wait is 1.7 on all eight cores, whether x was waited for 1.6 us or 3.3. It depends on more: in the kernels without the v stage's edit, or with the gain on VectorE, it is 0.5 to 0.6 and the stretch 65.5 instead of 65.9, which I didn't trace. 1.74 - 0.87 + 1.45 = 2.3 is near the 2.47 measured.

**Front, 1.3 forecast, nothing measured.** On core 0 x of chunk 2 was there at 12.66 where I said 11.6, and the first product of step 7 began at 29.02 where I said 28.4. The failed step is "x 2 to 7 come up to 2.6 us sooner": x 2, 3 and 5 came 1.2, 1.3 and 0.9 sooner. One of my signs of being wrong is there too, a wait of 0.5 for u weights at 13.7 us. ScalarE's timeline, core 0, against [rows 3]:

```profile
9.48 1.06 ACT L322 ACTIVATE arena<-arena 128x1024 bf16<-128x1024 f32 x1 [3.54 <-DMA arena<-x_p]
...
12.66 1.06 ACT L322 ACTIVATE arena<-arena 128x1024 bf16<-128x1024 f32 x1 [2.03 <-DMA arena<-x_p]
```

x of chunk 1 itself came 1.75 us later, 9.48 for 7.73. So the 2.6 was partly given back ahead of x 2. `colG` may not be the cause: in this trace the packets of the u weights also begin earlier and run beside x 1. Which of the two it is wasn't tried. The 1.57 us still left at step 7 (30.59 to 29.02), less the 0.85 of the moved products (8 x 0.1 is nearer that than the 0.9 I wrote), is the 0.7 us seen on core 0. But the v stage began between 86.0 and 86.9 on the mean of the cores in seven executions with this front, and between 86.3 and 86.9 in five with the old one; both sets average 86.6. I read a gain out of a stretch whose own spread from execution to execution is 0.9 us.

**Sum.** 15.4 was right for core 0 (15.5), with the merge blocks and the v stage 0.75 and 0.5 above their terms and the front and the residual rows 0.6 and 0.5 below them: luck in part. The metric follows the slowest core of each execution. In the profiled one of after that is core 2, 1.1 us behind core 0: 0.4 in the front and 0.8 in the GLU steps, where VectorE's piece stood still. That is where the 1.1 us are missing. Three other executions, 1080.6 to 1080.8, are 0.6 to 0.8 above the forecast. And a sum taken from the core with the longest waits and the fallen clock counts these in full, while the mean of the cores won 13.0.

## What to carry to other kernels

Where a wait for a DMA differs from core to core, read it, and the clock behind it, on all cores: its removal is worth the step down to the new slowest core, not the wait of the old one. An edit made alone can lengthen a wait further on, and a clock fall can hang on that; so look at every stretch, not only at the one that was changed. A product moved from a full TensorE to another engine is worth its columns, 0.22 us for 512; count what the receiving engine has to spare. If it is GpSimd, look which VectorE instructions with both inputs in SBUF fall beside its own, on every core. Take a start that varies by a microsecond between executions as no place for a gain of one.

## What the runs showed of the hardware that I had not expected

- VectorE and GpSimd exclude each other in both directions: 1.22 us became 3.35 and 0.41 became 1.55 on VectorE, 0.55 became 1.43 and 1.59 on GpSimd, in each case as much as the other's instruction still had to run, or nearly. Once, on core 2 of after, a VectorE piece that takes some 0.6 elsewhere stood 9.29 us, through sixteen GpSimd pieces in a row.
- Whether TensorE's clock falls after a pause isn't told by the pause: on 32 cores it fell after pauses of 2.3 to 4.2 us in 19 and stayed after 2.2 to 3.5 in 13, and in the v stage alone it fell on three of seven cores behind the same wait of 2.1. Where it fell, that cost 1.7 us.
- ScalarE writes 512 columns of bias into PSUM in 0.59 us, no more than it needs for a Gelu of 512 into SBUF, 0.59.
